# Several first products issued together, split norm passes, and four steps moved, in a two-block transformer kernel

## The chip, the core and the metric

The kernel runs on one NeuronCore of a Trainium2 chip. Its engines are TensorE (PE), VectorE (DVE), ScalarE (ACT), GpSimd (POOL) and SyncE (SP), each with its own instruction stream; they are ordered against each other by semaphores alone. The metric is the device time of one execution in microseconds, the median of several runs.

## The reference, cut to what matters

256 rows of width 1024 go through two layers of a first block and one layer of a second block, all in float32.

```python
def first_block(x, ...):                      # twice (DEPTH = 2)
    h = _swiglu(x, ffn_w1[l, 0], ffn_w3[l, 0], ffn_w2[l, 0])
    x = _layernorm(ALPHA * x + 0.5 * h, ln_g[l, 0], ln_b[l, 0])
    h = _mixer(x, l, ...)                     # z = x @ w_in: u, v, q, k, val, gates
    x = _layernorm(ALPHA * x + h, ln_g[l, 1], ln_b[l, 1])
    h = _swiglu(x, ffn_w1[l, 1], ffn_w3[l, 1], ffn_w2[l, 1])
    x = _layernorm(ALPHA * x + 0.5 * h, ln_g[l, 2], ln_b[l, 2])

def second_block(x, c, ctx, ...):             # once
    h, hc = modulate(rmsnorm(x), ...), modulate(rmsnorm(ctx), ...)
    ...                                       # neighbourhood attention o_na, gated linear attention o_g
    o_gla = rmsnorm(o_g, gla_norm_g) * silu(og)
    y = sigmoid(m_a) * (o_na @ w_br_na) + sigmoid(m_b) * (o_gla @ w_br_gla)
    x = x + g1 * (y @ w_o)
    h2 = modulate(rmsnorm(x, norm2_g), sh2, sc2)
    x = x + g2 * swiglu(h2, w_gate, w_up, w_down)
```

## The kernel before

**Products.** Every float32 operand of a large product is held as a high half (type fp32r) and the rest as a low half, and each product is three: high x high, high weight x low x, low weight x high x. Weights come in chunks of up to 1 MB into three `raw` buffers (SP, `load`), and each chunk is cut in parts of 128 x 1024. ACT copies a part to `whi` (line 1444) and DVE subtracts it to `wlo` (line 1883); there are four buffers of each, so a part can be split when the part four before it has been used. The class `Weights` fixes the place of each split in the order of ACT and DVE: `take` splits up to four parts ahead, `more(k)` splits k more at once. A load of chunk c waits until the low parts of chunk c - 3 are made, or until PE has read a whole chunk of the modulation.

**Two forms of products.** `gemm_a` makes one output of 128 x 256 in one PSUM bank from 8 k-blocks (24 products; lines 733, 734, 736). With `coming` it runs all high products first, then the low weights, then the low x (lines 718, 721, 724), asking for each block of x as it comes. `gemm_b` makes 128 x 512 outputs (lines 756, 758, 759), tile by tile; `tail` parts are held and run bank by bank at the end, `between` is called between its steps, `head` parts are held at the start.

**Norms.** After each down or out projection comes `layernorm(j)`, j = 0 to 5 (j = 0, 1, 2 in layer 0). DVE adds the four banks to X (line 1948), takes statistics (1950, 1952, 1954), subtracts the mean (1957) and scales (1960), first tile t = 0, then t = 1; POOL takes the power -1/2 between (line 2512). PE turns X (`turn_x`, line 814) and between the two tiles multiplies a whole chunk of the modulation (`modulation_half`, line 854); ACT copies the turned tile to XTh (1452) and DVE subtracts it to XTl (`low_x`, line 1908). j = 0 and 3 lead to the mixer, whose first product is V (`gemm_b`, 8 parts, tail 3, head 2); j = 1, 2, 4 lead to an FFN, whose first parts run with `coming`; j = 5 leads to the second block, whose first product is `vg` with X needed only from its third tile on.

**The mixer's table.** POOL loads and masks the table `ws` (line 2521); PE turns it (line 933) at call 5 of `between` in V, just before the tail.

**The second block.** `g10` turns the rows of the gated linear attention; DVE makes `og` (2362) from them and then the low half (2355) of ACT's copy (1776), four times. POOL makes the attention's bias from loaded tables (`bias`, lines 2611 and 2614), the first two after the power of the gated rows. `y` is a chain of DVE (2419), POOL (2638), ACT (1776) and DVE (2355), eight times; then `wo` makes 8 outputs, then the second RMS norm gives h2 (DVE 2442, ACT 1847, DVE 2438) and the last FFN starts.

`warm` and `settle` are products and turns whose result nobody reads.

## Time and profile before

| | before |
|---|---|
| runs | 1783.6, 1785.64, 1789.44 us, median 1785.64 |
| profiled execution | 1787.88 us, span 1786.1 us |
| PE busy | 1759.3 us (98%), 12755 products |
| PE weight loads | 1604.1 us (90%) |
| DVE, ACT, POOL busy | 1142.4 (64%), 864.1 (48%), 217.7 us (12%) |
| DMA | 334.71 MB, mean 187 GB/s |

An engine's busy time is the union of its instructions; PE's products are pipelined and their ends are modelled, so that the distance from one start to the next says more than a duration. An idle time in brackets is that of the engine before the instruction, with the instruction that ended it. Which instruction that was is inferred from semaphores.

### The profile page before, as it was taken

What the parts mean: (1) busy time and instruction counts of PE and PEld (TensorE: products, weight loads), DVE (VectorE), ACT (ScalarE), POOL (GpSimd) and SP (SyncE); (2) the same over time, 40 slices, a digit from 0 to 9 for tenths busy, and PEclk for the clock granted to TensorE, in tenths of its full rate; (3) what the DMA queues carried; (4) which work ended last, traced back from release to release, by engine and by line L of the source; (5) the groups of instructions that cost most, each with busy time, mean ns of one, the idle gap of its engine ahead of it and who ended that gap; (6) DMA issues with size and microseconds to landing.
All of it is one profiled execution on the core that took longest, in us unless ns stands there. A gap on an engine that the chain in (4) does not pass through costs nothing. (4 is left out here: it accounts for less than half of the span.)

```text
span 1786.1 us, 31142 instructions
## 1 busy us (share of the span) xinstructions
PE 1759.3 (98%) x12755; PEld 1604.1 (90%) x12755; DVE 1142.4 (64%) x1803; ACT 864.1 (48%) x1412; POOL 217.7 (12%) x284
## 2 busy tenths in 40 slices
PE   9999999999999999999999999999999999999999
PEld 9998699999899879997899997999768877889999
DVE  5774667776777466656586876676647455655553
ACT  5453344664444435443446653545436355445543
POOL 2000122211000000001222211000003243200000
PEclk9999999999999999999999999999999999999999
DMA  8585666445667557755765456676435333356663
GB/s 294 190 271 181 218 220 222 143 151 195 198 211 259 190 192 234 235 189 163 263 214 189 139 179 215 200 259 209 148 128 134 92 95 105 119 164 190 191 198 107
DMA packets 257518, 334.71 MB, mean 187 GB/s; under 512 B 15210, under 2 KB 217168, under 8 KB 257376
## 3 DMA queue, kind: packets, MB, share of 16 engines
q1 hardware_dynamic: 251312, 317.42, 54.7%
q0 software_dynamic: 6064, 15.31, 2.7%
q8 instruction: 101, 1.65, 0.4%
q14 instruction: 41, 0.34, 0.1%
HBM read 327.45 MB, written 1.05 MB: 184 GB/s over the span
## 5 line engine op out<-in xcount | busy, mean ns | idle before, releaser
L1883 DVE TENSOR_TENSOR wlo<-raw,whi 128x1024 fp32r<-128x1024 f32 x549 | 670.8, 1228 | 351.4 <-ACT whi L1444 346.8
L1444 ACT ACTIVATE whi<-raw 128x1024 fp32r<-128x1024 f32 x549 | 572.7, 1051 | 419.1 <-PE bank L759 223.2
L733 PE MATMUL bank<-XTh,whi 128*128 128x256 f32 x1984 | 555.6, 280 | 0.0
L736 PE MATMUL bank<-XTh,wlo 128*128 128x256 f32 x1984 | 551.7, 278 | 0.0
L734 PE MATMUL bank<-XTl,whi 128*128 128x256 f32 x1984 | 551.4, 278 | 0.0
L733 PEld LDWEIGHTS bank<-XTh,whi 128*128 128x128 f32 x1984 | 373.5, 188 | 2.3
L736 PEld LDWEIGHTS bank<-XTh,wlo 128*128 128x128 f32 x1984 | 374.3, 189 | 0.5 <-DVE wlo L1883 0.4
L734 PEld LDWEIGHTS bank<-XTl,whi 128*128 128x128 f32 x1984 | 372.9, 188 | 0.0
L733 PE MATMUL bank<-HCh,whi 128*128 128x256 f32 (+2 forms) x880 | 251.8, 286 | 0.6 <-DVE tmp L2419 0.6
L734 PE MATMUL bank<-HCl,whi 128*128 128x256 f32 (+2 forms) x880 | 247.6, 281 | 0.0
L736 PE MATMUL bank<-HCh,wlo 128*128 128x256 f32 (+2 forms) x880 | 247.3, 281 | 0.0
L733 PEld LDWEIGHTS bank<-HCh,whi 128*128 128x128 f32 (+1 forms) x880 | 165.9, 189 | 16.1 <-issue 12.5
L734 PEld LDWEIGHTS bank<-HCl,whi 128*128 128x128 f32 (+1 forms) x880 | 165.6, 188 | 1.8
L736 PEld LDWEIGHTS bank<-HCh,wlo 128*128 128x128 f32 (+1 forms) x880 | 165.7, 188 | 1.7
L758 PE MATMUL bank<-wlo,ffn1Hh 128*128 128x512 f32 x264 | 103.1, 391 | 0.4
L756 PE MATMUL bank<-whi,ffn1Hh 128*128 128x512 f32 x264 | 102.9, 390 | 0.0
L759 PE MATMUL bank<-whi,ffn1Hl 128*128 128x512 f32 x264 | 102.8, 390 | 0.0
L2512 POOL TENSOR_TENSOR rs<-rs,half 128x1 f32<-128x1 f32 x12 | 18.3, 1522 | 666.0 <-DVE rs L1954 666.0
L756 PE MATMUL bank<-whi,XTh 128*128 128x512 f32 x192 | 75.1, 391 | 0.7 <-ACT XTh L1452 0.7
L758 PE MATMUL bank<-wlo,XTh 128*128 128x512 f32 x192 | 75.1, 391 | 0.3
L759 PE MATMUL bank<-whi,XTl 128*128 128x512 f32 x192 | 74.9, 390 | 0.0
L758 PEld LDWEIGHTS bank<-wlo,ffn1Hh 128*128 128x128 f32 x264 | 49.6, 188 | 11.8 <-DVE wlo L1883 1.7
(344 smaller groups left out, 2362.2 us busy)
## 6 DMA issues: line engine op xcount, KB each, us to landing
raw<-in_ffn_w_dram SPq DMA_DIRECT2D x131, 1024.0 KB, 5.2
raw<-in_w_in_dram SPq DMA_DIRECT2D x76, 1024.0 KB, 5.2
raw<-in_w_mod_dram SPq DMA_DIRECT2D x24, 1024.0 KB, 5.1
raw<-in_w_branch_dram SPq DMA_DIRECT2D x16, 1024.0 KB, 5.1
raw<-in_w_out_dram SPq DMA_DIRECT2D x12, 1024.0 KB, 4.9
raw<-in_w_ffn_gate_dram SPq DMA_DIRECT2D x11, 1024.0 KB, 5.1
raw<-in_w_ffn_up_dram SPq DMA_DIRECT2D x11, 1024.0 KB, 5.0
raw<-in_w_ffn_down_dram SPq DMA_DIRECT2D x8, 1024.0 KB, 5.0
```

What stands on the lines that cost most here:

```text
L733: e.matmul(o, hi[:, k, w0:w0 + nc_], xh, start=first and k == 0, stop=False)
L734: e.matmul(o, hi[:, k, w0:w0 + nc_], xl, start=False, stop=False)
L736: m = e.matmul(o, lo[:, k, w0:w0 + nc_], xh, start=False, stop=last and k == nk - 1)
L756: e.matmul(o[:, :], xh, hi[:, k, s], start=kk == 0, stop=False)
L758: e.matmul(o[:, :], xh, lo[:, k, s], start=False, stop=False)
L759: m = e.matmul(o[:, :], xl, hi[:, k, s], start=False, stop=kk == nparts * nk - 1)
L1444: e.activation(hi_part(n), raw_part(n), ACTF.Copy).then_inc(WHI.did(n), 1)
L1883: e.tensor_tensor(lo_part(n), raw_part(n), hi_part(n).bitcast(F32), ALU.subtract).then_inc(WLO.did(n), 1)
L2512: e.tensor_tensor(rs[:, t, 1:2], rs[:, t, 0:1], nhalf, ALU.pow).then_inc(PLN.did(("rs", j, t)), 1)
```

## The change

1. **Norms** (DVE `layernorm`): tile 1's first add comes before tile 0's scaling; each scaling pass is made in two halves of 512 columns, and PE turns each half when it is there. For j = 0, 3 `low_x(t=0, c=0)` comes before the last pass. Both further weight splits come before the other `low_x`. For j = 5 (`turn=False`) one weight split is moved ahead of the last pass, so one more is made before the row norms.
2. **Banks**: for j = 0, 3 X is turned into banks 0 to 3 (before 0, 1, 2, 7), and the modulation's row uses bank 6 (before 3).
3. **First parts of each FFN** (`gemm_pair`): two outputs at once, in the order high of both, low weights of both, low x of both.
4. **V's first two parts** (`gemm_b`, `start`): for each tile high of both parts, low weights of both, low x of both.
5. **The mixer's table** is turned at call 6, between the two tiles of V's tail.
6. **og and y**: the low half of og(h) follows og(h + 1); that of y(m) follows na(m + 2) instead of na(m + 1).
7. **wo** (`first_three`): three outputs in three banks at once; k = 0 to 5 of all three products first, then k = 6, 7.
8. **h2** has a buffer of its own (in KNT, free by then) in place of a ring of four; DVE makes all eight h2 first and then the eight low halves.
9. **Biases** 0 and 1 are made before the powers of the keys.

```diff
+            def gemm_pair(outs, X, coming):
+                held = [w.take() for _ in outs]
+                for n, o in zip(held, outs):
+                    for k in range(8):
+                        coming(k, XHI)
+                        q.wait_ge(WHI, n)
+                        e.matmul(o, hi_part(n)[:, k, :], X(k)[0], start=k == 0, stop=False)
+                for n, o in zip(held, outs):
+                    q.wait_ge(WLO, n)
+                    for k in range(8):
+                        e.matmul(o, lo_part(n)[:, k, :], X(k)[0], start=False, stop=False)
+                for n, o in zip(held, outs):
+                    for k in range(8):
+                        coming(k, XLO)
+                        m = e.matmul(o, hi_part(n)[:, k, :], X(k)[1], start=False, stop=k == 7)
+                    w.give_back()
+                    m.then_inc(MM.did(("w", n)), 1)
...
+                def start(held, ti):
+                    t = tiles[ti]
+                    for p, n in enumerate(held):
+                        ready(p, t, XHI)
+                        q.wait_ge(WHI, n)
+                        for c in range(nb):
+                            if p == 0:
+                                empty(banks[ti][c])
+                            e.matmul(bank[banks[ti][c]][:, :], X(p, t)[0], hi_part(n)[:, 0, c * 512:(c + 1) * 512], start=p == 0, stop=False)
...
-                    if calls[0] != 5:
+                    if calls[0] != 6:
...
+                    outs = [bank[(32 + i) % 3][:, 0:T] for i in range(3)]
+                    for i in range(3):
+                        empty((32 + i) % 3)
+                    for product in (high, low_weight, low_y):
+                        for n, o in zip(held, outs):
+                            for k in range(6):
+                                product(n, o, k)
+                    for i, (n, o) in enumerate(zip(held, outs)):
+                        for product in (high, low_weight, low_y):
+                            for k in (6, 7):
+                                m = product(n, o, k)
+                        w.give_back()
+                        m.then_inc(MM.did(("w", n), ("wo", i)), 1)
...
+                def scale(t):
+                    if t and not turn:
+                        w.more(1)
+                    q.wait_ge(PLN, ("rs", j, t))
+                    q.wait_ge(DLN, ("g", j, t))
+                    for c in range(2):
+                        xv = X[:, t, c * 512:(c + 1) * 512]
+                        e.scalar_tensor_tensor(xv, xv, rs[:, t, 1:2], gb[:, 1, c * 512:(c + 1) * 512], ALU.mult, ALU.add).then_inc(
+                            DLN.did(("x", j, t, c), ("x", j, t)), 1)
+                for c in range(2):
+                    add(0, c)
+                    stats(0, c)
+                center(0)
+                add(1, 0)
+                scale(0)
+                stats(1, 0)
+                add(1, 1)
+                stats(1, 1)
+                center(1)
+                if j % 3 == 0:
+                    low_x(j + 1, 0, 0)
+                scale(1)
                 w.more(1)
                 w.take_whole()
+                g, h = NORMS[j]
                 if turn:
+                    w.more(1)
+                    if j % 3 == 0:
+                        if h:
+                            mod_columns(g, 6)
+                        low_x(j + 1, 1, 0)
+                    else:
+                        low_x(j + 1, 0, 0)
+                        low_x(j + 1, 1, 0)
+                        if h:
+                            mod_columns(g, 3)
+                    low_x(j + 1, 0, 1)
+                    low_x(j + 1, 1, 1)
...
-                    low("og", h, OGl[:, h, :], s[:, :], OGh[:, h, :])
+                    if h:
+                        low("og", h - 1, OGl[:, h - 1, :], tmp[t2r.slot["og", h - 1]][:, :], OGh[:, h - 1, :])
...
-                    if m:
-                        low("y", m - 1, HCl[:, m - 1, 0:T], tmp[t2r.slot["y", m - 1]][:, :], HCh[:, m - 1, 0:T])
+                    if m > 1:
+                        low("y", m - 2, HCl[:, m - 2, 0:T], tmp[t2r.slot["y", m - 2]][:, :], HCh[:, m - 2, 0:T])
...
+                q.wait_ge(SMALL, ("ns", 15))
                 for k in range(8):
-                    ring_free(q, t2r, ("h2", k))
...
-                    if k:
-                        low_h2(k - 1)
-                low_h2(7)
+                for k in range(8):
+                    low_h2(k)
...
-                powers("k", 4)
...
+                for h in range(2):
+                    bias(h)
+                powers("k", 4)
```

## Rows read from the trace of the kernel before

**Rows 1.** The page's first part: busy us, share of the span, instructions.
```profile
PE 1759.3 (98%) x12755; PEld 1604.1 (90%) x12755; DVE 1142.4 (64%) x1803; ACT 864.1 (48%) x1412; POOL 217.7 (12%) x284
```
**Rows 2.** PE's waits, whole span: us in total, times, longest.
```profile
PE bank L758 <- DVE wlo L1883: 3.6, 2, 2.0
```
**Rows 3.** A stretch: length, busy (instructions) of PE, PEld, DVE, ACT, POOL; granted clock; DMA.
```profile
1301.50:1307.50 6.00, 6.00 (x19) 4.66 (x19) 0.17 (x1) 0.00 (x0) 0.00 (x0) 0.50 0.53 175
```
**Rows 4.** Line 733's products alone in two stretches of an FFN.
```profile
660.00:715.00 55.00, 43.72 (x157) 1.00 0.73 235
1110.00:1165.00 55.00, 44.69 (x162) 1.00 0.69 226
```
**Rows 5.** Timeline of PE around norm 2: start, us, instruction, count [idle before].
```profile
649.93 1.09 PE L814 MATMUL bank<-cst,X 128*128 128x128 f32 x8 [1.02 <-DVE X L1960]
...
651.32 1.17 PE L718 MATMUL bank<-XTh,whi 128*128 128x256 f32 x8 [0.19 <-ACT XTh L1452]
...
654.69 0.71 PE L724 MATMUL bank<-XTl,whi 128*128 128x256 f32 x4 [0.83 <-DVE XTl L1908]
...
657.12 1.10 PE L724 MATMUL bank<-XTl,whi 128*128 128x256 f32 x8
```
**Rows 6.** Timeline of DVE around norm 2.
```profile
648.59 1.28 DVE L1960 SCALAR_TENSOR_TENSOR X<-X,rs,gb 128x1024 f32<-128x1024 f32 x1 [0.44 <-POOL rs L2512]
649.79 1.22 DVE L1883 TENSOR_TENSOR wlo<-raw,whi 128x1024 fp32r<-128x1024 f32 x1
```
**Rows 7.** Timeline of PE around norm 0 and in V.
```profile
201.56 1.09 PE L814 MATMUL bank<-cst,X 128*128 128x128 f32 x8 [1.07 <-DVE X L1960]
203.35 0.47 PE L756 MATMUL bank<-whi,XTh 128*128 128x512 f32 x1 [0.69 <-ACT XTh L1452]
...
218.54 1.09 PE L933 MATMUL bank<-cst,G 128*128 128x128 f32 x8 [1.16 <-POOL G L2521]
```
**Rows 8.** Timeline of ACT in V.
```profile
217.29 2.01 ACT L1444 ACTIVATE whi<-raw 128x1024 fp32r<-128x1024 f32 x2 [6.97 <-DMA raw<-in_w_in_dram]
```
**Rows 9.** DMA queues from 205.7 to 209.5: packets, MB, share of 16 engines.
```profile
q1 hardware_dynamic: 1, 0.00, 0.3%
```
**Rows 10.** Timeline of PE after norm 5.
```profile
1294.31 0.50 PE L758 MATMUL bank<-wlo,HCh 128*128 128x512 f32 x1 [1.65 <-DVE wlo L1883]
...
1300.67 0.50 PE L758 MATMUL bank<-wlo,HCh 128*128 128x512 f32 x1 [1.99 <-DVE wlo L1883]
...
1302.67 1.86 PE L864 MATMUL bank<-cmb,spare 2*128 2x2 f32 x8
```
**Rows 11.** Timeline of PE at the attention's first scores.
```profile
1447.37 1.50 PE L1292 MATMUL bank<-KNT,QNT 64*128 64x512 f32 x2 [2.15 <-DVE tmp L2362]
```
**Rows 12.** Timeline of DVE ahead of them.
```profile
1439.70 5.92 DVE L1883 TENSOR_TENSOR wlo<-raw,whi 128x1024 fp32r<-128x1024 f32 x3
```
**Rows 13.** Timeline of POOL, 1386 to 1455.
```profile
1392.94 6.49 POOL L2589 TENSOR_TENSOR sv<-sv,half 128x8 f32<-128x8 f32 x4 [11.08 <-DVE sv L2252]
...
1438.65 1.02 POOL L2614 TENSOR_TENSOR BT<-BT,nm 128x384 f32<-128x384 f32 x1
...
1440.72 1.86 POOL L2614 TENSOR_TENSOR BT<-BT,nm 128x384 f32<-128x384 f32 x1
```
**Rows 14.** Timeline of PE at the first output of wo.
```profile
1562.53 0.38 PE L718 MATMUL bank<-HCh,whi 128*128 128x256 f32 x1 [2.27 <-ACT HCh L1776]
```
**Rows 15.** Timeline of DVE in y and wo.
```profile
1559.56 1.23 DVE L1883 TENSOR_TENSOR wlo<-raw,whi 128x1024 fp32r<-128x1024 f32 x1 [0.45 <-ACT whi L1444]
...
1561.37 0.42 DVE L2419 TENSOR_TENSOR tmp<-bank,G 128x256 f32<-128x256 f32 x1
...
1572.51 0.48 DVE L2426 SCALAR_TENSOR_TENSOR XTf<-bank,sh,XTf 128x256 f32<-128x256 f32 x1 [0.40 <-PE bank L736]
```
**Rows 16.** Timeline of ACT at h2.
```profile
1598.64 0.51 ACT L1847 ACTIVATE HCh<-tmp,sh 128x256 fp32r<-128x256 f32 x1 [0.28 <-DVE tmp L2442]
```
**Rows 17.** Timeline of PE at h2.
```profile
1603.07 1.07 PE L724 MATMUL bank<-HCl,whi 128*128 128x256 f32 x8
```

121 lines of the change are left out of this document (70 added, 51 removed).

## Prediction

> **What bounds the kernel now.** I read the page first: TensorE (PE) is busy 98% of a span of 1786.1 us [rows 1]. The change adds no product and takes none away, so it can win only time in which PE stands still or runs slowly, and lose only by making new such time. Next the list of PE's waits [rows 2], the longest of which is 3.6 us for low weights, and then the timeline around each wait. Two things in it are small in the list and larger in fact. A stretch of waits is followed by a stretch in which the granted clock is 0.50, that is 1.2 instead of 2.4 GHz: 6.0 us of it after 1301.5 [rows 3], and the same reading of 0.50 stands over the 2.5 us after 1448.5 and after 1564.5; the two shorter ones last 3.4 us from end to end, the first 6.8. And products of 256 columns run at one of two paces at full granted clock: line 733 issued 157 in 55 us in one stretch and 162 in another [rows 4], so three products (733, 734, 736) take 350 or 340 ns.
>
> **Norms ahead of an FFN (j = 2, 4; j = 1).** At j = 2 PE has done the half of the modulation at 648.91, stands 1.02 us until VectorE (DVE) has written all of X, turns it, starts the FFN's first part at 651.32, waits 0.83 us for XTl, and is through two parts at 657.12 + 8 x 0.118 = 658.06 [rows 5]. In the new order DVE adds tile (1,0) while POOL takes the power of tile 0, which fills a gap of 0.45 us like that before 648.59; the last pass, 1.28 us, is two halves of 0.64, and PE may turn the first half after one [rows 6]. So x(1, half 0) is there at 648.59 - 0.5 + 0.7 = 648.8 instead of 649.87, ahead of PE at 648.91. PE turns from 648.95 to 650.0, ACT copies half by half behind it, and the first product goes at 650.2. DVE now splits two weights (1.22 us each [rows 6]) ahead of the four XTl pieces (0.6 each), so the last piece lands at 649.4 + 2.4 + 2.4 = 654.2. The pair of parts asks for it only after 32 + 4 products: 650.2 + 36 x 0.1133 = 654.3, just late enough. The pair ends at 650.2 + 48 x 0.1133 = 655.65; with 0.1 for two small waits the gain is 658.06 - 655.75 = **2.3**. j = 4 has the same three waits (1.03, 0.34 and 0.61 in its own timeline rows, which repeat this pattern): **2.2**. At j = 1 two products more precede the modulation, PE waits only 0.3 us for XTl: **0.3**. The first FFN of all starts from the first two weight halves as they land; the pair wants the second one 16 products earlier: **-0.2**, bounded by 0 and one split's 1.22.
>
> **V after j = 0 and j = 3, and the mixer's table.** At j = 0 PE waits 1.07 us for X and 0.69 us before V's first product, which the list puts down to XTh but which needs XTl too; then 1.16 us at line 933 for POOL's table [rows 7]. New: the piece XTl(0,0) is made in POOL's gap ahead of the last pass, x(1) ends at 201.15, and V starts at 201.75 instead of 203.35. Its first eight products need the second low weight at 203.05, and DVE has it at 201.15 + 2 x 1.2 = 203.5: 0.4 lost. V's third part starts at 207.6 instead of 209.05: 1.45 gained. The table's turn comes one tile (18 products of 0.227 = 4.1 us) later, and its waits, 1.3 and 1.8 us start to start in the two layers, lie well inside that. What is late next: V's last two parts. ACT gets their chunk from DMA only at 217.29 [rows 8], PE would now be at the first of them at 215.8 + 0.7, and before it was the table's wait that hid this. The chunk was issued at 205.05, and in 205.7 to 209.5 queue 1 moved one packet [rows 9] while POOL's five loads ran on queue 0. If it lands when it did, layer 0 keeps only 0.6 of 2.8 us and layer 1 0.5 of 1.8. But its issue waits for the second low weight, which is 1.45 us earlier, ahead of POOL's first packets; I take a landing about 1.2 us earlier: **1.5** (0.6 to 2.8) in layer 0, **1.3** (0.5 to 1.8) in layer 1. j = 3 itself had no wait and keeps none: its columns free bank 6 before V's second tile asks for it.
>
> The Trainium skill (DMA: Bandwidth & Descriptors, "Queues, rings and completion order") says that each DMA engine takes turns between its queues packet by packet. The silence of queue 1 in the row speaks against even turns here; by that rule the chunk, issued earlier, would land up to 3 us earlier and both layers would keep all, 4.6 instead of 2.8.
>
> **Norm j = 5 and the gate projections.** PE waits for low weights at 1294.31 (1.65 idle, 2.0 start to start) and at 1300.67 (1.99, 2.15 start to start) [rows 10]: the first one is made only after X, the fourth after the row norms. New: the first is made in POOL's gap, 1290.8 to 1292.0, ahead of PE at 1292.16, at the cost of nothing that PE waits for (X ends at 1293.2 as before, its users come 10 us later). The second lands at 1294.3, PE wants it at 1293.75: 0.6 lost. Third and fourth are at 1295.5 and 1296.65, ahead of PE. The fourth product group ends at 1298.2 instead of 1302.65, where line 864 begins [rows 10]: **4.4** (3.5 to 4.4). The 6.8 us at half clock that follow two idle stretches of 2 us in 6.4 us cost 3.4; only 0.6 idle is left there, less than the 1.02 at j = 2, after which the clock stayed full: **3.4** (0 or 3.4).
>
> **The gated rows (og) and the biases.** PE waits 2.15 us (2.3 start to start) at 1447.37 for og(1) [rows 11]. og(0) begins when DVE is through three low weights that took 5.92 us [rows 12], where three take 3.66 at the 1.22 of [rows 6]: POOL did bias(0) to bias(2) in that time, at 1.86 us an operation, where the one at 1438.65 took 1.02 [rows 13]; they slow each other. Two of the three move to the stretch before the keys' powers, where POOL stood idle 11.08 us [rows 13]; their DMAs, issued at 1346 and 1356, landed by 1365, 16 us before, so the four operations (4.1 us) hold nobody. There they run beside eight products KI, EN of DVE, after which it idles 4 us. Then the weights end at 1443.3, og(0) and og(1) need 0.8 more since low(0) is behind them: 1444.2, and PE is there at 1445.2. Gain **2.3** (1.0 if the biases did not slow DVE); the half clock after it, 3.4 us, costs 1.6: **1.6** (0 or 1.6).
>
> The Trainium skill (SBUF — State Buffer, "Who interferes with whom") says that of a GpSimd operation and a VectorE one with two SBUF inputs the later one blocks fully. The 5.92 agrees (3.66 and two blocks of 1.0 are 5.7), and by it the moved biases could hold DVE at 1382 by up to 4.1 us, which its idle time there still covers.
>
> **y, the first three outputs.** PE stands 2.27 us before 1562.53 for the last high halves, some 4 us with the waits around it [rows 14]. "low(m-2) instead of low(m-1)" saves nothing: the chain from pair to pair is na, POOL's sum, ACT's copy, ACT's weight, DVE's weight, na, 3.92 us, and the weight split before na(6) ended a wait on ACT [rows 15], not on a low half. So na(7) still ends at 1561.8, and only then may PE start the three outputs, since it now asks for all three banks. From there all goes without a wait: 72 products end at 1561.85 + 8.16 = 1570.0, where the third output before was taken by DVE at 1572.51 [rows 15], so ended at 1572.2. But PE now idles 2.9 us in one piece, so I expect the half clock again, at 1.6: 0.6 to 2.2, taken as **1.0**. Weights of outputs 4 to 6 come free up to 4 us later and have as much in hand.
>
> **h2.** ACT's eight copies came in steps of 0.79 us, the last ending at 1599.15, and PE followed them until both parts were through at 1603.07 + 8 x 0.113 [rows 16, 17]; DVE alternated h2 and low. With all h2 first the step is 0.45, the last at 1597.0, before PE (from 1596.74 on) has done its seventh product; the lows end at 1599.1, PE asks for the first at 1600.4. The pair ends at 1602.2 instead of 1604.0: **1.85**.
>
> **Sum.** 2.3 + 2.2 + 0.3 - 0.2 + 1.5 + 1.3 + 4.4 + 3.4 + 2.3 + 1.6 + 1.0 + 1.85 = 21.95 us. The profiled execution took 1787.88 for a span of 1786.1; it is 2.2 above the median, 1785.64, of runs from 1783.6 to 1789.44. 1787.88 - 21.95 = 1765.9 for a run like it, and against the median 1785.64 - 21.95 = 1763.7, which I predict.
>
> **Rivals.** (a) The clock still falls at the three places, because PE is little busy there with narrow products and transposes: 5.0 less, 1768.7. For it: the falls came after 2 us idle in all. Against it: waits of 1.0 at j = 0, 2 and 4 brought none. (b) The weight chunk of V lands as before: 1.7 less, 1765.4; it rests on the silence of queue 1. (c) The pace. Which of the two a stretch gets seems to be set by how its first products fall after a break: the slow one of j = 2 began at a wait that goes, and 67 us of FFN run in it (2.6 us to win), the one of j = 4 turned fast at such a wait (85 us, 3.3 to lose). One flip for the worse and none for the better: 1767 to 1769. This is also the way to **slower**: 10.8 ns in three products [rows 4], or by the means of the same rows up to 5 ns a product, over 8592 products is at most 43 us; it outweighs the gain and 5.4 us more only if over 5500 of them go from fast to slow, which would give 1791 and up. Nothing in the trace asks for it, since the stretches whose lead-in has no wait keep it. (d) The change doesn't do what it says: for the low halves of y I hold this already; if the biases were not what slows DVE, og(1) comes at 1446.5 and 1.3 and the clock's 1.6 are gone: 1766.6.
>
> **How the numbers follow.** The sum within 4 us: 0.60. (a), alone or with part of (b): 0.15, (b) or (d) alone: 0.07. (c) as one or two bad flips, with or without (a): 0.13, up to 1774. Slower: 0.02; more gained than 1757: 0.03. Upper ends of the unknown terms (V 2.8 + 1.8, y 2.2, pace 2.6) give 1763.7 - 5.6 = 1758, and with run to run spread 1755; lower ends with (a) and a bad flip 1774. Range 1755 to 1774. A difference of 0.3%, 5.4 us, is about what a measurement of this kernel can tell from none: faster 0.92 (all cases but the worst tenth of (a) and (c) together), same 0.06, slower 0.02.
>
> **What would show it.** Right: no wait of PE over 0.3 us at j = 2 and 4 and none on X; V's last two parts start with a wait on wlo or whi in place of line 933's; no half clock near 1293 and 1440, one near 1550; three low weights in 3.5 us before og. Wrong: a half clock at the first two places, a new wait on DVE at the second part of a pair, or a long FFN stretch with 157 instead of 162 products in 55 us.

## The result and the profile after

| | before | after |
|---|---|---|
| median of the runs, us | 1786.12 (1783.6 to 1789.44, 4 runs) | 1768.74 (1766.0 to 1769.61, 4 runs) |
| profiled execution, us | 1787.88 | 1766.0 |
| its span, us | 1786.1 | 1764.2 |

The ratio of the times is 0.990, with a 95% interval of 0.988 to 0.992: 17.4 us less. A later series, with 9 runs of the kernel before and 5 of the changed one, gave 1787.43 and 1770.82, a ratio of 0.990 (0.989 to 0.992) and 16.6 us.

The prediction was 1763.7 us, from a sum of 21.95 us. The two profiled executions lie 21.9 us apart. That looks exact and isn't: the steps that the sum names gave 15.4 us, and the rest came from the pace of the 256-column products, for which the sum counts nothing. The later executions below show this.

First the page of the changed kernel, its row for TensorE (PE: busy us, share, instructions). It answers [rows 1].

```profile
PE 1749.7 (99%) x12755; PEld 1595.4 (90%) x12755; DVE 1143.4 (65%) x1815; ACT 862.5 (49%) x1412; POOL 218.0 (12%) x284
```

**Norm 2 and norm 5.** The timelines of PE and of VectorE (DVE) around norm 2 answer [rows 5, 6]; columns as there.

```profile
644.35 3.60 PE L903 MATMUL bank<-raw,csil 128*2 128x512 f32 x8
647.89 1.32 PE L863 MATMUL bank<-cst,X 128*128 128x128 f32 x8
649.28 2.26 PE L753 MATMUL bank<-XTh,whi 128*128 128x256 f32 x16
...
653.19 1.98 PE L761 MATMUL bank<-XTl,whi 128*128 128x256 f32 x16
...
647.08 1.41 DVE L2049 SCALAR_TENSOR_TENSOR X<-X,rs,gb 128x512 f32<-128x512 f32 x2 [0.44 <-POOL rs L2623]
648.41 2.36 DVE L1962 TENSOR_TENSOR wlo<-raw,whi 128x1024 fp32r<-128x1024 f32 x2
650.68 2.48 DVE L1987 TENSOR_TENSOR XTl<-bank,XTh 128x512 fp32r<-128x512 f32 x4
```

No row of PE has a bracket, so it waits for nothing from the half of the modulation (L903) to the end of the pair. The four XTl pieces end at 653.16. The pair reads the first two from 653.19 on and needs the other two only four products later, at 653.64. So the cover that the prediction worked out at 0.1 us (654.2 against 654.3) has 0.5 left over. At norm 5 all that is left of the waits of [rows 10] is this one.

```profile
1283.94 0.50 PE L781 MATMUL bank<-wlo,HCh 128*128 128x512 f32 x1 [0.47 <-DVE wlo L1962]
```

**Layer 0's V.** Rows of PE, ScalarE (ACT), DVE and GpSimd (POOL) there, against [rows 7, 8].

```profile
217.10 0.50 PE L781 MATMUL bank<-wlo,XTh 128*128 128x512 f32 x1 [0.76 <-DVE wlo L1962]
219.14 0.79 PE L781 MATMUL bank<-wlo,XTh 128*128 128x512 f32 x1 [1.07 <-DVE wlo L1962]
223.33 1.03 PE L982 MATMUL bank<-cst,G 128*128 128x128 f32 x8
...
214.73 2.01 ACT L1523 ACTIVATE whi<-raw 128x1024 fp32r<-128x1024 f32 x2 [5.92 <-DMA raw<-in_w_in_dram]
215.82 3.26 DVE L1962 TENSOR_TENSOR wlo<-raw,whi 128x1024 fp32r<-128x1024 f32 x2 [5.57 <-ACT whi L1523]
216.11 1.89 POOL L2632 TENSOR_SCALAR_AFFINE_SELECT G<-G 128x1024 f32<-128x1024 f32 x1 [12.29 <-DMA G<-in_lam_dram]
```

The table's turn (L982) no longer waits. Two waits for V's low weights stand in its place, 1.83 us in all against 1.16 before. The chunk was there at 214.73, which is 2.56 us earlier than in [rows 8] and not 1.2 as predicted. But its two low weights took 3.26 us instead of 2.4.

**The last projection.** PE ahead of the first three outputs and in them, and DVE before that, against [rows 14, 15].

```profile
1541.08 4.18 PE L1417 MATMUL bank<-HCh,whi 128*128 128x256 f32 x18 [3.09 <-DVE tmp L2531]
...
1538.64 1.23 DVE L1962 TENSOR_TENSOR wlo<-raw,whi 128x1024 fp32r<-128x1024 f32 x1 [1.15 <-ACT whi L1523]
1539.78 0.42 DVE L2531 TENSOR_TENSOR tmp<-bank,G 128x256 f32<-128x256 f32 x1
```

The one long wait came as predicted, 3.09 us instead of 2.9, and the last pair's two products with the gates (L2531), of which the first is shown and the second ends at 1540.8, stand behind a low weight which DVE waited for. The first 18 products take 4.18 us where 2.04 is full speed. The table of stretches says why (length, PE busy, PEld, DVE, ACT, POOL, then the granted clock, DMA share, GB/s).

```profile
219.10:222.50 3.40, 3.36 (x8) 2.69 (x9) 1.23 (x1) 0.70 (x1) 0.00 (x0) 0.50 0.85 275
1540.10:1546.90 6.80, 5.82 (x27) 5.85 (x28) 3.62 (x7) 1.78 (x3) 1.71 (x2) 0.50 0.17 39
```

These are the only two half clocks (1.2 of 2.4 GHz) of this execution ahead of its last microsecond. The ones of [rows 3] at norm 5 and the one behind the gated rows are gone.

**Gain by stage.** This is the start of the same product of PE in both traces, and how far the distance between the two grew over each stage.

| stage | predicted, us | measured, us |
|---|---|---|
| start | -0.2 | -0.26 |
| norm 0, V and table, layer 0 | 1.5 | -1.34 |
| V and table, layer 1 | 1.3 | 1.20 |
| j = 1 | 0.3 | 0.40 |
| j = 2, j = 4 | 2.3, 2.2 | 2.10, 1.97 |
| j = 5: waits, clock | 4.4, 3.4 | 4.07, 2.47 |
| og: waits, clock | 2.3, 1.6 | 2.22, 1.57 |
| y, first three outputs | 1.0 | -0.67 |
| h2 | 1.85 | 1.67 |
| sum | 21.95 | 15.4 |
| everything between, by pace | 0 | 6.5 |

At j = 5 waits and clock are parted where the prediction parts them, at the start of line 864's products. The half clock began 1.5 us before that, at 1301.2. Parted there, the waits gave 3.4 us and the clock 3.1.

Before, 3061 products of 256 columns were followed by the next one after about 117.8 ns instead of 113.3; after, 1515 were: (3061 - 1515) x 4.5 ns = 7.0 us. What turned fast lies mostly in the stretches 53.7 to 101.5, 394.9 to 459.6, 654.9 to 722.3 and 871.2 to 945.0 of the trace before.

### The profile page after: what moved, and what is told of

It reads as the page before. It is cut to its first block, busy times and chain, and to the rows that moved or that the text cites. A ratio compares the mean times of both kernels' runs of the same rounds, so it can differ in the third digit from the quotient of the medians.

```text
span 1764.2 us, 31152 instructions
## 1 busy us (share of the span) xinstructions
PE 1749.7 (99%) x12755; PEld 1595.4 (90%) x12755; DVE 1143.4 (65%) x1815; ACT 862.5 (49%) x1412; POOL 218.0 (12%) x284
## 3 DMA queue, kind: packets, MB, share of 16 engines
q8 instruction: 101, 1.65, 0.4%
## 4 chain that ended last, share of the span: by engine, by line
PE 91%; DVE 4%; DMA 2%; ACT 2%; issue 1%; POOL 0%; DVEq 0%; SPq 0%
PE bank L737 19%; PE bank L740 19%; PE bank L738 19%; PE bank L781 7%; PE bank L782 7%; PE bank L779 7%; DVE wlo L1962 2%; DMA raw<-in_w_in_dram 1%; ACT whi L1523 1%; PE bank L903 1%; PE bank L1341 1%; PE bank L1363 1%; PE bank L885 1%; PE bank L753 1%; PE bank L1029 1%
## 5 line engine op out<-in xcount | busy, mean ns | idle before, releaser
L737 PE MATMUL bank<-HCh,whi 128*128 128x256 f32 (+2 forms) x864 | 246.1, 285 | 0.6 <-DVE tmp L2531 0.6
L738 PE MATMUL bank<-HCl,whi 128*128 128x256 f32 (+2 forms) x864 | 241.9, 280 | 0.0
L740 PE MATMUL bank<-HCh,wlo 128*128 128x256 f32 (+2 forms) x864 | 241.8, 280 | 0.0
L737 PEld LDWEIGHTS bank<-HCh,whi 128*128 128x128 f32 (+1 forms) x864 | 161.7, 187 | 15.7 <-issue 12.1
L738 PEld LDWEIGHTS bank<-HCl,whi 128*128 128x128 f32 (+1 forms) x864 | 161.8, 187 | 1.8
L740 PEld LDWEIGHTS bank<-HCh,wlo 128*128 128x128 f32 (+1 forms) x864 | 161.7, 187 | 1.7
L781 PE MATMUL bank<-wlo,XTh 128*128 128x512 f32 x176 | 69.9, 397 | 2.4 <-DVE wlo L1962 2.1
L779 PE MATMUL bank<-whi,XTh 128*128 128x512 f32 x176 | 69.3, 394 | 0.0
L782 PE MATMUL bank<-whi,XTl 128*128 128x512 f32 x176 | 69.2, 393 | 0.0
L1555 ACT ACTIVATE ffn1Hh<-ffn1Hf 128x256 fp32r<-128x256 f32 x66 | 27.6, 418 | 68.2 <-DVE ffn1Hf L2007 68.2
```

The lines of the kernel that those rows point to most:

```text
L737: e.matmul(o, hi[:, k, w0:w0 + nc_], xh, start=first and k == 0, stop=False)
L738: e.matmul(o, hi[:, k, w0:w0 + nc_], xl, start=False, stop=False)
L740: m = e.matmul(o, lo[:, k, w0:w0 + nc_], xh, start=False, stop=last and k == nk - 1)
L779: e.matmul(o[:, :], xh, hi[:, k, s], start=kk == 0, stop=False)
L781: e.matmul(o[:, :], xh, lo[:, k, s], start=False, stop=False)
L782: m = e.matmul(o[:, :], xl, hi[:, k, s], start=False, stop=kk == nparts * nk - 1)
```

## Experiments

Two parts of a span turned out to change from one execution of the same program to the next. So each span is also given with both taken out: the half clock (what each product of 256 or 512 columns that starts in one takes beyond 113.3 or 226.7 ns, at most that much again) and the slow pace (what each product of 256 columns whose successor starts 116 to 120 ns later takes beyond 113.3). I call the rest the bare span. Products of other widths that run at half clock are left in it: this is 1.3 us of the first trace of before, most of it at norm 5.

| kernel | span | half clock | slow pace (products) | bare span |
|---|---|---|---|---|
| before | 1786.1 | 5.0 | 13.6 (3061) | 1767.5 |
| before_again | 1783.9 | 4.2 | 11.4 (2554) | 1768.3 |
| changed | 1764.2 | 4.2 | 6.8 (1515) | 1753.2 |
| after_again | 1761.1 | 0.0 | 7.3 (1641) | 1753.8 |
| after_third | 1769.8 | 4.3 | 12.0 (2692) | 1753.5 |
| table_back | 1767.2 | 4.6 | 6.4 (1446) | 1756.2 |
| select_behind | 1766.0 | 4.4 | 9.0 (2025) | 1752.6 |
| gb_late | 1767.2 | 2.7 | 13.9 (3132) | 1750.6 |
| biases_back | 1771.5 | 4.3 | 10.4 (2329) | 1756.8 |
| wo_before | 1763.4 | 1.6 | 8.4 (1886) | 1753.5 |
| split_behind | 1764.7 | 3.1 | 10.4 (2345) | 1751.2 |
| norm5_back | 1774.7 | 6.0 | 10.5 (2357) | 1758.2 |
| filled | 1768.1 | 1.5 | 12.2 (2726) | 1754.4 |
| both | 1762.2 | 0.0 | 12.6 (2842) | 1749.6 |

The same kernel gives the same bare span within 0.8 us, while its spans lie up to 8.7 us apart.

### The same kernels again

> The changed kernel once more, to see which parts of the 21.9 us between the two profiled executions belong to the program and which to one execution. In the profiled execution of the changed kernel 1515 products of 256 columns ran at the slow pace (about 117.8 ns from start to start instead of 113.3), before 3061; that is 7.0 us of the 21.9. Theory A (the pace is set by how the program's products fall, so it repeats): the same stretches are slow within some 100 products, and the span is 1764.2 within 0.7. Theory B (the pace is drawn anew in each execution): other stretches are slow, some 3 us more of them, since three of the four times of the changed kernel lie 2.3 to 3.6 us above the profiled one. Under both, the half clock starts at about 219.1 (3.4 us) and 1540.1 (6.8 us).

> The kernel before once more. Two executions of the changed kernel differed in their half clocks: one had them at 219.1 and 1540.1, the other none at either place, with the same waits. So the 5.0 us that the prediction counts for the clock (3.4 at norm 5, 1.6 at the gated rows) rest on one execution of the kernel before. Theory A (after two waits of 2 us the clock always falls): the half clocks stand at 1301.2 (6.8 us) and 1448.0 (3.4 us) again. Theory B (such waits only make a fall possible, and it is drawn anew in each execution): at least one of the three at 1301, 1448 and 1564 is missing or new ones stand elsewhere, while all waits of PE agree within 0.3 us. The long stretches of 256-column products at the slow pace (53 to 101, 228 to 302, 395 to 460, 655 to 722, 871 to 945) recur in part: those at 228 to 302 under both theories of the pace, since every execution so far has it.

The changed kernel had no half clock at either place, though PE waited 1.80 us in V and 3.10 us ahead of the first output. Its stretches at the two places of the first trace, and the outputs:

```profile
218.90:222.30 3.40, 3.40 (x20) 2.90 (x20) 1.22 (x1) 1.23 (x2) 0.00 (x0) 1.00 0.86 282
1540.30:1547.10 6.80, 6.80 (x58) 6.80 (x59) 2.64 (x4) 1.78 (x3) 0.91 (x2) 1.00 0.31 82
...
1540.29 2.36 PE L1417 MATMUL bank<-HCh,whi 128*128 128x256 f32 x18 [3.10 <-DVE tmp L2531]
```

The kernel before had all three again, the first one half as long as in [rows 3]:

```profile
1302.00:1305.40 3.40, 3.40 (x10) 2.73 (x10) 0.17 (x1) 0.00 (x0) 0.00 (x0) 0.50 0.58 225
1445.40:1448.80 3.40, 3.40 (x13) 2.48 (x12) 1.91 (x5) 1.32 (x3) 0.00 (x0) 0.51 0.10 31
1561.40:1564.80 3.40, 3.40 (x19) 3.40 (x18) 1.71 (x2) 0.79 (x2) 0.00 (x0) 0.50 0.18 25
```

So for after_again my expectation that both theories share (the half clocks come again) was wrong, and for before_again theory A held as to the places and not as to the length. A wait makes a fall likely and doesn't decide it. The waits themselves don't all repeat either: the table's in layer 1 was 1.60 us in the first trace of before and 0.91 in the second. The span of after_again, 1761.1 us, is neither theory's: nearly as few products were slow as in the first trace, and the half clocks were missing. The pace repeats in part. The stretch from 228 to 302 is slow in 13 of the 14 traces (in table_back it is fast), the one of norm 2's FFN (655 to 722) in 4, the one from 871 to 945 in 10, the one that begins behind j = 4 in 3. A long stretch changes its pace at a break. Some of these breaks are another instruction, as at 53.9 before, where a transpose of the modulation came in. At others two products of 256 columns start 0.2 to 0.4 us apart with nothing between them, as at 92.6 and 538.0 in the first trace of the changed kernel, and the traces don't show why.

### The table back, and the select behind the low weights

```diff
-                    if calls[0] != 6:
+                    if calls[0] != 5:
```

> The mixer's table goes back one tile, to where it was before the change; all else as changed. Theory A (the step of the prediction that failed is not the table's move but what was late next: V's sixth and seventh weight, whose low halves are written while GpSimd's select runs beside VectorE): in layer 0 PE reaches the table's turn at about 215.2 and waits until the select ends at about 218.0, 2.9 us, finds both low weights there afterwards, and the two waits of 0.76 and 1.07 us are gone; the half clock stays or gets longer; the end of V (measured at the start of the first product after it) comes 0.5 to 1.5 us later than in the changed kernel. In layer 1 about 1 us later. Theory B (the move itself costs, since the table was hidden where it was): V ends 1 us or more earlier than in the changed kernel and the half clock at 219 is gone.

```profile
220.10 1.97 PE L982 MATMUL bank<-cst,G 128*128 128x128 f32 x8 [4.12 <-POOL G L2632]
...
218.42 1.63 POOL L2632 TENSOR_SCALAR_AFFINE_SELECT G<-G 128x1024 f32<-128x1024 f32 x1 [13.90 <-DMA G<-in_lam_dram]
```

PE waits 4.12 us for the table and for nothing else in V. The stage is 2.9 us longer than in the changed kernel and 4.5 longer than in after_again. Theory A held. My price was too low: the last rows of the table landed later in this execution (the select began at 218.42), and the half clock lasted 6.8 us instead of 3.4. The move of the table gains, and what failed is what comes behind it.

```diff
                 q.wait_ge(MIN[l], "in")
+                q.wait_ge(WLO, parts.index((first_qk[l] - 1, 1)))
                 e.affine_select(out=ws, in_=ws, compare_op=ALU.is_ge, fill=0.0, base=0, pattern=[[0, 8], [-1, 128]],
```

> GpSimd's select over the mixer's table waits until VectorE has written the low half of V's last weight but one chunk's second part; all else as changed. This takes the two operations apart (they ran together: two low weights in 3.26 us instead of 2.36, the select 1.89 us instead of 1.1). Theory A (they slow each other): the two low weights take 2.36 us, the second is there at about 218.2 instead of 219.1, PE's wait of 1.07 us there falls to 0.2 to 0.4, the select runs from 218.2 to 219.3, well before the table's turn at about 222; V ends 0.8 us earlier, and 2.3 earlier if the half clock at 219.1 goes with the wait. Theory B (the low weights are slow for another reason, the DMA's traffic into SBUF): they still take 3.2 us and V ends as it did, within 0.2.

```profile
218.96 0.50 PE L781 MATMUL bank<-wlo,XTh 128*128 128x512 f32 x1 [0.16 <-DVE wlo L1962]
...
216.55 2.36 DVE L1962 TENSOR_TENSOR wlo<-raw,whi 128x1024 fp32r<-128x1024 f32 x2 [5.64 <-ACT whi L1523]
219.05 1.10 POOL L2633 TENSOR_SCALAR_AFFINE_SELECT G<-G 128x1024 f32<-128x1024 f32 x1 [14.55 <-DVE wlo L1962]
```

Apart, the two low weights take 2.36 us and the select 1.10; together they took 3.26 and 1.89. PE's second wait fell from 1.07 to 0.16, V ended 0.8 us earlier at equal clock and 2.4 with the half clock gone: theory A. The times of the rows fit one waiting for all of the other. The select, released at 216.11, would run from the end of the first low weight at 217.0 to 218.0, and the second low weight from there to 219.1. In after_again the order was the other way round, and there the low weights alone pay for it:

```profile
215.51 1.10 POOL L2632 TENSOR_SCALAR_AFFINE_SELECT G<-G 128x1024 f32<-128x1024 f32 x1 [11.85 <-DMA G<-in_lam_dram]
215.60 3.22 DVE L1962 TENSOR_TENSOR wlo<-raw,whi 128x1024 fp32r<-128x1024 f32 x2 [5.54 <-ACT whi L1523]
```

The 0.8 us rests on these rows more than on the length of the stage (norm 0, V and the table). At equal clock that is 30.7 us here and 31.4 to 31.5 in the changed kernel, but 30.9 to 32.3 in the five further kernels that leave V alone. That this execution had no half clock is not proof of anything, since after_again had none either.

### V's norm rows loaded late

```diff
-                q.wait_ge(DLN, ("x", 3 * l, 1))
-                load_gb((1, 5)[l], I["sgu_ln_g"][l], I["sgu_ln_b"][l])
                 mixer(l)
...
                                 channel_multiplier=1).then_inc(PMX.did(("ws", l)), 1)
+                q.wait_ge(DLN, ("x", 3 * l, 1))
+                load_gb((1, 5)[l], I["sgu_ln_g"][l], I["sgu_ln_b"][l])
```

> GpSimd's two loads of V's norm rows, spread over 128 partitions (1 MB in all), are issued behind the select instead of ahead of the table's three loads; all else as changed. Theory A (queue 1 is silent behind these spread loads, and V's chunk of 1 MB lands late through them): the chunk lands 2 to 4 us earlier than 214.7, PE's two waits for V's low weights (0.76 and 1.07 us) and the half clock at 219.1 go, and V ends 3.3 us earlier (1.8 of waits, 1.5 of clock). Theory B (the chunk is late for itself, by its issue): it lands within 0.5 us of 214.7, and only the table's rows come earlier; V ends up to 0.8 earlier through the select that then runs by itself.

These are the issue of V's weight chunk in the changed kernel and in this one (line, KB, us from issue to landing), then POOL, DVE and PE of this one.

```profile
raw<-in_w_in_dram SPq DMA_DIRECT2D x1, 1024.0 KB, 11.9
```

```profile
raw<-in_w_in_dram SPq DMA_DIRECT2D x1, 1024.0 KB, 8.6
...
209.65 1.12 POOL L2632 TENSOR_SCALAR_AFFINE_SELECT G<-G 128x1024 f32<-128x1024 f32 x1 [8.58 <-DMA G<-in_lam_dram]
212.67 2.42 DVE L1962 TENSOR_TENSOR wlo<-raw,whi 128x1024 fp32r<-128x1024 f32 x2 [0.82 <-ACT whi L1523]
219.37 1.04 PE L982 MATMUL bank<-cst,G 128*128 128x128 f32 x8
```

The chunk, issued at the same time, landed at 211.56 instead of 214.70. PE has no wait from 211 to 226, and the stage is 4.1 us shorter than in the first trace of the changed kernel (2.5 at equal clock), 2.8 shorter than in the kernel before: the upper bound that the prediction gave for it. The kernel with both edits, below, has the same length there. Theory A held, though the estimate of the gain (3.3) was 0.8 low.

The Trainium skill (DMA: Bandwidth & Descriptors, "Queues, rings and completion order") says that each DMA engine takes turns between its queues packet by packet. A chunk whose flight grows from 8.6 to 11.9 us by the loads on the other queue agrees with such a sharing over the whole flight. The 3.8 us of [rows 9] with one packet don't, and no run here shows why.

### The biases back beside the gated rows

```diff
-                for h in range(2):
-                    bias(h)
                 powers("k", 4)
...
+                    if n > 1:
+                        bias(n - 2)
```

> GpSimd's first two biases go back beside the gated rows; all else as changed. Theory A (the biases and VectorE's low weights slow each other): three low weights take 5.9 us again instead of 3.7, og(1) comes 2.2 us later, PE waits 2.0 to 2.3 us at the gate projections, and everything behind is 2.2 us later than in the changed kernel, 3.8 if the clock falls there. Theory B (the wait went because low(0) now stands behind og(1), 0.4 to 0.6 us, and the low weights are slow by themselves): the wait is back to 0.5 us at most.

```profile
1429.01 5.92 DVE L1962 TENSOR_TENSOR wlo<-raw,whi 128x1024 fp32r<-128x1024 f32 x3
...
1435.77 1.12 PE L1341 MATMUL bank<-KNT,QNT 64*128 64x512 f32 x2 [1.25 <-DVE tmp L2472]
```

In the changed kernel the same three low weights read as follows, and PE waits nowhere between 1415 and 1430:

```profile
1422.59 3.49 DVE L1962 TENSOR_TENSOR wlo<-raw,whi 128x1024 fp32r<-128x1024 f32 x3
```

They are back at 5.92 us, to the last digit that of [rows 12], and PE is 1.95 us later from there on. Theory A held. Its 1.6 us of clock didn't come: no half clock follows in this execution. The bare span is 3.3 us longer; 1.3 of that lies elsewhere and is not explained.

### Norm 5's first low weight back behind X

```diff
                 def scale(t):
-                    if t and not turn:
-                        w.more(1)
```

> At norm j = 5 the first low weight of the gate projections is written behind the whole of X again instead of in the gap in which GpSimd takes the power; all else as changed. This undoes the edit that the prediction counts highest, 4.4 us of waits and 3.4 of half clock (measured between the first two traces: 4.07 and 2.47). Theory A (one weight earlier shifts all four): PE waits 1.6 to 1.7 us for the first low weight and 1.9 to 2.1 for the fourth, 4.0 to 4.4 us from start to start in place of 0.6, and a half clock of 3.4 or 6.8 us follows within 8 us of the first wait, as in both executions of the kernel before. Theory B (the other edits of norm 5, the order of stats and of the columns, carry part of it): 3 us or less.

```profile
1285.74 0.51 PE L781 MATMUL bank<-wlo,HCh 128*128 128x512 f32 x1 [1.25 <-DVE wlo L1962]
1292.11 0.50 PE L781 MATMUL bank<-wlo,HCh 128*128 128x512 f32 x1 [1.98 <-DVE wlo L1962]
...
1293.10:1299.90 6.80, 6.80 (x21) 5.27 (x21) 0.17 (x1) 0.00 (x0) 0.00 (x0) 0.50 0.48 154
```

Both waits are back and the half clock with them. PE is 6.2 us later behind norm 5: 3.0 by waits and 3.2 by the clock. Both are parted where the half clock begins, and so parted the whole change gave 3.4 and 3.1. So one low weight, moved ahead of DVE's last pass over X, carries 3.0 of the 3.4 us of waits; the first wait is 1.25 here and 1.65 in [rows 10], so the other 0.4 comes from DVE's new order of adding and stats. The number lies on the edge that I set between the theories; the mechanism is A's. The bare span is 4.7 us longer. About 1 us of what goes beyond the 3.0 is narrow products at half clock; the rest lies elsewhere and is not explained.

### The last projection

```diff
-                first_three()
-                for n in range(3, 8):
+                for n in range(8):
...
-                    gemm_a(bank[b][:, 0:T], xx, ("wo", n))
+                    gemm_a(bank[b][:, 0:T], xx, ("wo", n), coming=y_ready if n == 0 else None)
```

> The first three outputs of the last projection go one by one again, each bank asked for only ahead of its own products, as before the change; all else as changed. Prediction: 1.0 us later than the changed kernel at the sixth output, from 2.6 less of waits and 1.6 of half clock. Measured so far: the changed kernel was 0.67 us slower there with a half clock of 6.8 us, so about 1.0 faster without. Theory A (2.6 us of waits are really saved; the clock took them back): PE's waits from the last pair on are 2.3 to 2.6 us longer than in the changed kernel, and it is 2.4 later than an execution of the changed kernel without a half clock, if it has none itself. Theory B (waiting for all three banks costs as much as it saves): within 0.5 us of that execution.

```profile
1541.21 0.38 PE L722 MATMUL bank<-HCh,whi 128*128 128x256 f32 x1 [2.27 <-ACT HCh L1825]
1542.08 0.58 PE L722 MATMUL bank<-HCh,whi 128*128 128x256 f32 x1 [0.49 <-ACT HCh L1825]
```

The waits from the last pair on are 4.9 us from start to start with some clock in them, against 4.0 in after_again (0.75 and 3.27), with a half clock of 3.4 us from 1542.1 on. The bare span is that of the changed kernel, 1753.5. With its own half clock taken out it is 0.4 us later than after_again, or 0.8 with the slow products taken out too, and theory A asked for 2.4. So it is theory B in the main: by itself the new order of the three outputs saves 0.4 to 0.8 us. From the same product at 1537 to the one at 1550 this kernel is 0.5 us faster than the changed one with its 6.8 us of half clock, and 2.0 us slower than after_again, 1.6 of which is its own half clock.

```diff
                 for m in range(8):
-                    if m % 2 == 0:
-                        w.take()
-                    else:
-                        w.give_back()
...
+                    if m % 2:
+                        w.take()
+                        w.give_back()
```

> VectorE writes each pair's low weight behind the pair's two products with the gates instead of ahead of them; all else as changed. In the changed kernel PE stands 3.09 us ahead of the first three outputs, until VectorE has taken the last pair at 1540.8; VectorE was free to take it at 1537.9, but first waited for ScalarE's high weight (1538.6) and wrote its low part (1.23 us). Theory A: the last pair is taken by 1538.6, PE's wait falls from 3.09 to 0.8 or 0.9 us, the waits of 0.58 us between pairs go too, and the time at the first output is 2.2 to 3.5 us less than in the changed kernel; with so short a wait no half clock follows, which gives 3.4 more against an execution that has it. Theory B (something else ends the wait, the high halves of y through GpSimd's sums): PE starts at about 1540.3 and gains 0.7 at most.

```profile
1544.21 2.31 PE L1417 MATMUL bank<-HCh,whi 128*128 128x256 f32 x18 [1.26 <-DVE tmp L2527]
...
1543.59 0.41 DVE L2527 TENSOR_TENSOR tmp<-bank,G 128x256 f32<-128x256 f32 x1
1543.92 1.41 DVE L1962 TENSOR_TENSOR wlo<-raw,whi 128x1024 fp32r<-128x1024 f32 x1
```

The wait fell from 3.09 to 1.26, the gain by the sixth output is 5.4 us against the changed kernel: 2.7 by waits and 2.7 by the half clock that this execution lacks there. Theory A held, with 0.4 us more wait than expected: the low half of y(5) ahead of the last pair took 0.95 us on DVE where 0.42 is usual, beside POOL's two sums (2.53 us where they took 1.71).

Then the wait was left as it was and filled, with 24 products that nobody reads:

```diff
+                    for i in range(24):
+                        e.matmul(bank[5][:, 0:T], ONh[:, 0, 0:128], ONh[:, 0, :], start=True, stop=True)
                     outs = [bank[(32 + i) % 3][:, 0:T] for i in range(3)]
```

> 24 products of 256 columns whose result nobody reads (2.72 us at 113.3 ns) stand ahead of the first three outputs, in the 3.1 us in which PE waits for the last pair; all else as changed, the wait itself included. In eight of the nine profiled executions so far that had an idle stretch of over 2 us there a half clock of 3.4 or 6.8 us followed; in the one whose idle stretch was 1.3 us none did. Theory A (it is the idle stretch that lets the clock fall): none here, and the first output starts when it did, within 0.2 us; the six groups of 48 products after it gain 1.6 to 3.2 us against an execution with the fall. Theory B (the fall comes from what ran before, narrow products among them, and would come anyway): a half clock within 3 us of 1541.

```profile
1544.36 3.04 PE L1428 MATMUL bank<-HCh 128*128 128x256 f32 x24
1547.62 1.62 PE L1417 MATMUL bank<-HCh,whi 128*128 128x256 f32 x12 [0.22 <-DVE tmp L2533]
...
1544.40:1551.20 6.80, 6.58 (x57) 6.41 (x56) 5.09 (x8) 2.84 (x5) 1.95 (x3) 1.00 0.38 132
```

The first output starts 3.37 us after the last product of the pairs, as in the changed kernel, and no half clock follows; by the sixth output this kernel is 2.7 us ahead of the first trace of the changed one. That agrees with theory A, in one execution. Over all traces, 10 of the 11 executions in which PE stood idle for over 2 us around the first outputs had a half clock behind it, and none of the 3 in which it was idle for 1.3 us at most or had filler products.

### Both good edits

The edits of gb_late and of split_behind in one kernel, and the changed kernel in the same series.

> The two edits that did best, together: V's norm rows loaded behind the select, and each pair's low weight written behind its two products with the gates. Each by itself gained, with half clocks and slow-pace products taken out of the span, 2.6 and 2.0 us against 1753.2 of the changed kernel (1750.6 and 1751.2). Theory A (they lie 1300 us apart and add up): 1748.6 so taken, and a median 4 to 8 us below the changed kernel's of the same call, the upper end where the half clocks at V and at the last projection go too. Theory B (what is gained early is given back at a later wait that was hidden): 1750.6 or more so taken, and at most 3 us.

> The changed kernel itself in the same call, as the measure for the one with both edits, and for its ratio to the kernel before. Its times so far are 1762.9 to 1769.6; before's are 1783.6 to 1793.0. Theory A (waits repeat within 1 us, half clocks and pace are drawn anew each time and spread the runs over some 7 us): median 1764 to 1769, and a third profile whose span without half clocks and slow-pace products is again 1753 to 1754. Theory B (the two executions differed for another reason): that figure lies elsewhere by more than 1.5 us.

The kernel with V's norm rows late and the low weights behind the pairs took 1759.59 us (1758.73 to 1763.98, 4 runs); its ratio to the kernel before is 0.985 (0.983 to 0.987), and it is 11.2 us below the changed kernel of the same series (1770.82). The bare span of 1749.6 lies midway between the two theories, 3.9 us below the changed kernel's where the two edits alone made 2.9 and 2.3. But this is not theory B's loss at a later wait. In V the kernel is as long as gb_late and in the last projection as split_behind. What is missing lies in the first 20 us, which neither edit touches: PE waited 0.84 us there for X from memory and 0.75 for a low weight, and at equal pace the stretch took 2.0 us more than in the first trace of the changed kernel. So the two edits add up, as in theory A.

The median gained more than the 4 to 8 that I expected. The changed kernel's own median, 1770.82, lies above the 1764 to 1769 expected for it, while its bare span is inside theory A's 1753 to 1754. The mean granted clock of the four runs with both edits was 0.999 to 1.000, that of the changed kernel's five 0.996 to 0.999; 0.003 less of clock is some 10 us at half speed, as in the first trace of the changed kernel, where it cost 4.2. Its profiled execution, with 2842 slow products, was its slowest run.

## Why the prediction was right, and where not

The range held, and the number was 5 us too low. By the accounts below, about 2.5 us of this are waits that brought less than counted, half of it in layer 0's V, and about 3 us are the clock; the pace gave some of it back. (The 3.6 us that the prediction calls the longest wait are two waits together, the longer of 2.0.)

**Norms (2.3, 2.2, 0.3) and h2 (1.85).** Right to 0.25 us each; here every start and end was built from durations of rows that are the same after.

**Norm 5 (4.4 + 3.4).** Together 7.8, measured 6.54. Half of the difference was counted twice: the 4.4 goes up to line 864 at 1302.65, and so has the first 1.5 us of the half clock in it, which cost 0.7, while the 3.4 prices all of it. The waits alone gave 3.4, near the lower bound of 3.5, and the clock 3.1. The step that reads 6.8 us of half clock as certain was too sure as well: in the second execution of the kernel before it lasted 3.4. But it stood there in all three executions with the two waits of norm 5, and in none of the eleven without. Rival (a), that the clock still falls there without the waits, is out.

**og (2.3 + 1.6).** Right, by the mechanism named: undoing it alone brings 5.92 and 1.95 us back. Rival (d) is out for the biases. The prediction held y's later low halves to be worth nothing; that was not tried by itself, but the chain it gave for that place (the low weight ahead of the pair ends the wait) is what split_behind shows.

**Layer 1's V and j = 3 (1.3).** 1.20 in the first trace, 0.9 and 0.35 in the two others of the changed kernel; inside the bounds in two of three. But the kernel before was itself 0.7 us shorter there in its second trace. Against the mean of its two the three gains are 0.9, 0.5 and 0, so that the agreement of 1.20 with 1.3 is in part luck.

**Layer 0's V (1.5).** Wrong by 2.8 us. The failed step is "I take a landing about 1.2 us earlier: 1.5". The landing itself was 2.5 earlier, better than assumed, and rival (b) is out; what fails is the way from the landing to the gain. The prediction lets the lateness of the chunk cost 1.3 of 2.8. Measured at equal clock, from gb_late with no wait (2.75 ahead of the kernel before) down to the changed kernel (0.25), the chunk costs 2.5. Of this 1.7 is still there in select_behind: even at 214.7 it is late, since ACT's copy and DVE's low weight take until 217.0 and PE is there at 216.3. The other 0.8 is what its arrival collides with: its low weights and POOL's select now start together and one waits for the other. Then, behind two waits of 0.76 and 1.07 us, the clock fell in the profiled execution, 1.5 us more; in after_third it didn't fall behind the same two. Without that fall the stage gave 0.3. The upper bound of 2.8 was to be had, by gb_late. In the section on the biases the prediction counts what DVE and POOL cost each other, and it didn't do so here. The Trainium skill (SBUF — State Buffer, "Who interferes with whom") says that a DVE operation with two SBUF inputs and a GpSimd one that reads SBUF exclude each other, and that who starts first decides which one is held up; the rows agree (217.0, 218.0, 219.1, and the reverse order in after_again).

**First three outputs (1.0).** Measured -0.67. The waits were as worked out: in after_again, without a half clock, the stage gave 1.75, and 2.0 with the slow products of both priced at the fast pace, near the upper end of 2.2. Only 0.5 of this is waits; the rest is the half clock of the kernel before, 1.5. The failed term is "the half clock again, at 1.6": it lasted 6.8 us in the first trace and cost 2.7. Of the ten traces with one there it lasted 6.8 us in five and 3.4 in five.

**Pace (rival c).** The prediction gave it 0.13 and only for the worse. It was the largest error of all in the pair of profiled executions, 6.5 us to the good, which hid the other misses. The medians leave 0.4 to 1.2 us for it (below), and the three traces of the changed kernel have 1515, 1641 and 2692 slow products. "Which of the two a stretch gets seems to be set by how its first products fall after a break" holds as to where it changes, but the same program draws it anew. The bare spans differ by 1767.9 - 1753.5 = 14.4 us. About 1 us of it is narrow products at half clock: the stages of the first pair, without the clock, sum to 13.4. The prediction has 16.95 besides its two terms for the clock, or 15.9 without the 0.7 counted twice and without 0.4 for a missing half clock at the last projection. Of the 5.0 counted for the clock, 4.7 were seen at norm 5 and og, but others came: in V, longer at the last projection, and at 1327. On average half clocks cost 4.6 us in the two traces of before and 2.8 in the three of the changed kernel. 14.4 + 1.8 is 16.2, where the medians show 17.4 and 16.6. The slower side, which needed 5500 products to flip, was never near.

## What to carry over

Before a wait is removed by bringing a transfer in earlier, list what starts when it lands: here the select and the low weights, which hold each other up, began within 0.3 us of each other. A load that nobody needs soon (V's norm rows, which landed at 209.2 and were not read before 260) belongs behind one that somebody waits for. Where a TensorE wait of over 2 us must stay, it can cost up to 3 us more by the clock; shorten it or fill it. A sum made against one profiled execution should name what in it is drawn anew each time, and be checked with a second profile of the same kernel before a few microseconds are believed.

## Not expected of the hardware

**A half clock without a wait.** In 6 of the 14 traces the clock fell at 1323 to 1331, where PE stands idle nowhere near. In all six the fall begins between 0.6 us ahead of the start of the last of eight products over 32 partitions and 1.2 us behind it. From the third trace of the changed kernel:

```profile
1323.31 3.69 PE L1183 MATMUL bank<-SO 32*128 32x512 f32 x8
1326.93 0.46 PE L737 MATMUL bank<-HCh,whi 128*128 128x256 f32 x1
...
1327.10:1330.50 3.40, 3.40 (x17) 3.40 (x18) 2.53 (x3) 1.57 (x2) 0.00 (x0) 0.50 0.18 69
```

Full-width products stand on both sides, so the narrow ones may act like a wait. In the two traces of before the clock did not fall there; it had fallen 32 to 35 us before these products. That doesn't explain it, since in norm5_back it had fallen 35 us before them and fell again. What makes the clock fall there was not tried: no run had these products made wide or taken away.

**Two paces at full clock.** The same line in the same stretch, 660 to 700 us, in the changed kernel and in the one with both edits (count, then minimum, median and maximum in ns, first and last start):

```profile
L740 PE MATMUL bank<-XTh,wlo x118: 276/276/276, 660.0 to 699.8; 128*128 128x256 f32 x118
```

```profile
L740 PE MATMUL bank<-XTh,wlo x114: 281/281/281, 659.9 to 699.9; 128*128 128x256 f32 x114
```

Every product of the stretch is 4 to 5 ns slower, at a granted clock of 1.00 in both. Over the 14 traces this is worth 6.4 to 13.9 us of the span, more than most edits here. What sets it was not found.
